# Attention units two at a time in every second group of the expert stream, with two buffers for their magnitudes

## The reference, cut to what matters

```
# stick-breaking attention, block i of 128 queries, keys 0 .. kv_len
z = einsum('bhqd,bhkd->bhqk', q_i, k_i) * scale
log_fail = where(mask, -softplus(z), 0.0)
later_fail = cumsum(log_fail, axis=3, reverse=True) - log_fail
w = where(mask, exp(log_sigmoid(z) + later_fail), 0.0)
outs.append(einsum('bhqk,bhkd->bhqd', w, v_i))
...
# experts, one block of 128 tokens; idx holds 128 experts for each token
u = expert_u[idx]
act = gelu(einsum('thkd,td->thk', u, tb))
return einsum('thk,thkd->td', g * act, expert_v[idx])
```

## Time and profile before

| what | value |
|---|---|
| median of the runs | 3309.58 us |
| the profiled execution: its own time | 3309.43 us |
| its span, first to last instruction | 3307.6 us |
| granted TensorE clock, mean | 0.959 |
| PE busy, share of the span | 2857.1 us, 86% |
| DVE, ACT, POOL busy | 2026.9, 1498.7, 1310.7 us |
| HBM traffic over the span | 345 GB/s |

### The profile page before, as it was taken

How to read it: one execution, slowest core, us unless ns; L and a number is a source line. 1 busy time by engine, 2 the same in 40 slices (tenths; PEclk the granted TensorE clock), 3 DMA queues, 4 the chain that set the end, 5 groups by cost and what they waited for, 6 DMA issues and landing times.

```text
span 3307.6 us, 33642 instructions
## 1 busy us (share of the span) xinstructions
PE 2857.1 (86%) x8606; PEld 1370.9 (41%) x8606; DVE 2026.9 (61%) x4767; ACT 1498.7 (45%) x3712; POOL 1310.7 (40%) x1134
## 2 busy tenths in 40 slices
PE   8899779997999879997999879998997689777776
PEld 5668634433453334433453334433452235322222
DVE  2111684895559655785559655795559655975444
ACT  3151153784446633674448733685332333232222
POOL 1000134544444434443444534444343444345553
PEclk9999889998999999998999989999998899999999
DMA  3541499999999999989998999989999899999998
GB/s 111 174 126 56 153 356 392 387 333 368 381 420 341 342 375 399 389 322 383 386 419 331 334 364 386 397 322 357 381 422 383 366 407 400 400 403 387 421 421 335
DMA packets 200267, 1143.70 MB, mean 346 GB/s; under 512 B 23585, under 2 KB 59761, under 8 KB 68737
## 3 DMA queue, kind: packets, MB, share of 16 engines
q0 software_dynamic: 147456, 1073.81, 81.7%
q1 hardware_dynamic: 52608, 67.67, 6.2%
HBM read 1126.31 MB, written 15.07 MB: 345 GB/s over the span
## 4 chain that ended last, share of the span: by engine, by line
PE 40%; DVE 23%; DMA 18%; issue 8%; ACT 6%; POOL 3%; POOLq 0%; DVEq 0%; SPq 0%; ACTq 0%
PE ps L1482 20%; DMA r_uv<-in_experts,r_wk 17%; DVE r_uv L1156 9%; PE ps L1260 5%; PE ps L1436 3%; PE ps L1419 3%; POOL r_uv L609 3%; PE ps L1221 2%; DVE r_wk L1094 2%; DVE r_wk L1092 1%; DVE r_wk L1095 1%; DVE r_wk L1000 1%; DVE r_wk L1003 1%; DVE r_wk L1009 1%; PE ps L1290 1%
## 5 line engine op out<-in xcount | busy, mean ns | idle before, releaser
L1482 PE MATMUL ps<-r_uv,r_wk 128*128 128x512 f32 x4096 | 1956.2, 622 | 376.2 <-ACT r_wk L838 371.4
L609 POOL DMA_INDIRECT r_uv<-in_experts,r_wk x1024 | 1199.2, 1171 | 1716.3 <-PE ps L1482 1385.5
L1156 DVE CUSTOM_DVE_ANT_0 r_uv<-r_uv,hncur 128x1024 f32<-128x1024 f32 x1024 | 1251.0, 1242 | 736.4 <-DMA r_uv<-in_experts,r_wk 726.0
L1482 PEld LDWEIGHTS ps<-r_uv,r_wk 128*128 128x128 f32 x4096 | 767.0, 196 | 1390.5 <-issue 877.8
L828 ACT ACTIVATE r_wk<-r_wk 128x2 f32<-128x2 f32 x512 | 104.4, 204 | 1294.3 <-DVE r_wk L1156 1292.6
L838 ACT ACTIVATE r_wk<-cst,r_wk 128x128 f32<-128x128 f32 x1024 | 356.0, 395 | 100.4 <-PE ps L1482 56.3
L834 ACT ACTIVATE r_wk<-r_wk 128x1 f32<-128x1 f32 x1024 | 246.2, 288 | 17.2
L828 ACT ACT_TABLE_LOAD x151 | 193.7, 1283 | 19.0 <-issue 16.4
L637 ACT ACT_TABLE_LOAD x147 | 188.6, 1283 | 6.6 <-PE ps L1412 1.9
L1436 PEld LDWEIGHTS ps<-r_wk,r_wq 128*128 128x128 f32 x1024 | 123.8, 192 | 27.0 <-issue 26.8
L1436 PE MATMUL ps<-r_wk,r_wq 128*128 128x128 f32 x1024 | 124.0, 275 | 0.0
(11 more groups left out here) (155 smaller groups left out, 2035.8 us busy)
## 6 DMA issues: line engine op xcount, KB each, us to landing
r_uv<-in_experts,r_wk POOLq DMA_INDIRECT x1024
r_wk<-lkv_dram SPq DMA_DIRECT2D x72, 128.0 KB
r_uv<-in_x SPq DMA_DIRECT2D x8, 512.0 KB, 3.6
hncur<-in_w_chunks SPq DMA_DIRECT2D x8, 512.0 KB, 3.9
h2cur<-in_w_chunks SPq DMA_DIRECT2D x8, 512.0 KB, 3.8
fnb<-in_w_chunks SPq DMA_DIRECT2D x8, 512.0 KB, 4.4
r_wo<-in_w_out SPq DMA_DIRECT2D x8, 512.0 KB, 5.1
r_wk<-in_x SPq DMA_DIRECT2D x8, 512.0 KB
```

What stands on the lines that cost most here:

```text
L609: g.indirect_dma_start(uv[:, k % NB, :], None, experts, bass.IndirectOffsetOnAxis(idxcur_u[:, k:k + 1], 0)).then_inc(rows_in[k % NB], 16)
L1156: v.tensor_tensor_reduce(uv[:, k % NB, 0:D], uv[:, k % NB, 0:D], hncur[:, :], 1.0, 0.0, ALU.mult, ALU.add, actv[:, k:k + 1]).then_inc(dott ...
L1482: last = t_.matmul(ps[:, i, :], diag[:, k % 4, :], uv[:, k % NB, D + 512 * i:D + 512 * i + 512], start=k == 0, stop=k == K - 1)
```

## The change

`LATE_AT` now starts two units in the same group, and the next two two groups later. In numbers: units 0 to 19 of block 0 started in groups 34, 35, 36, 37, 38, 40, ... 56 and start in 34, 34, 36, 36, ... 52, 52; in blocks 1 and 2 the 14 units end in group 46 in place of 56, in blocks 3 and 4 the 18 units end in group 50 in place of 56. `laz` becomes two buffers, chosen by u % 2, so ACT may write the logs of a unit while DVE has not yet read those of the one before. The room for it comes from a new buffer of 512 words and from letting `pos` and `posf` share theirs (the conversion is done in place).

```
-LATE_AT = {f: [34 + 24 * u // len(units) for u in range(len(units))] for f, (g, units) in LATE.items()}
+LATE_AT = {f: [34 + 2 * (u // 2) for u in range(len(units))] for f, (g, units) in LATE.items()}
...
-        pos = grid(pos_v.bitcast(U32), PH)
+        pos = grid(posf_v.bitcast(U32), PH)
...
+        laz1_v = sb("laz1", 512)
         laz_v, lw0_v = parts(qT_v, [512, 512])
-        laz = grid(laz_v, 2)
+        laz = (grid(laz_v, 2), grid(laz1_v[:, :], 2))
...
             def late_logs(b, first, u):
-                if u >= 1:
-                    gate(act, "act", lsp_ready, ub + u)
+                if u >= 2:
+                    gate(act, "act", lsp_ready, ub + u - 1)
                 act.wait_ge(lz_ready, ub + u + 1)
-                unit_logs(u, laz[0:r, :, c0:GW], bank(u, r, c0))
+                unit_logs(u, laz[u % 2][0:r, :, c0:GW], bank(u, r, c0))
...
             def late_softplus(b, first, u):
-                softplus(u, lsp[0:r, u % 2, :, :], laz[0:r, :, c0:GW], bank(u, r, c0), c0, own_)
+                softplus(u, lsp[0:r, u % 2, :, :], laz[u % 2][0:r, :, c0:GW], bank(u, r, c0), c0, own_)
```

More of the change, by code:

```diff
@@ L241, in block_program @@
         small = sb("small", 64)
-        r_wk = sb("r_wk", 13216)
+        r_wk = sb("r_wk", 13088)
         (pT_v, ssb_v, sq_v, qT_v, hs, hnn, in_v, topv_v, topi_v, topf_v, cs_v, ci_v,
-         lw1_v, tops_v, pos_v, posf_v, idxf, idxn, gn, actv, gel, idxcur, gcur, diag_v) = parts(r_wk, [
+         lw1_v, tops_v, posf_v, idxf, idxn, gn, actv, gel, idxcur, gcur, diag_v) = parts(r_wk, [
              2048, 2048, D, D, D, D, 512 + P + 512, 256, 256, 256, PH * NC, PH * NC,
-             512, K, K, K, K, K, K, K, K, K, K, 4 * P])
+             512, K, K, K, K, K, K, K, K, K, 4 * P])
         TOP_AT = 2 * 2048 + 4 * D + 512 + P + 512
```

## The result

The changed kernel takes 3379.6 us (median of 4 runs, 3376.1 to 3382.9) against 3311.6 us for the kernel before on the same chip: a ratio of 1.0205, 95% interval 1.0187 to 1.0223. The forecast was 3343.5 us, its own range 3318 to 3370, and the wide range up to rival C 3304 to 3383. The direction was right; 34.1 us more were forecast and 68.0 came, so the forecast was half of it and the measured time lies above its own range. The profiled execution took 3382.93 us, 73.5 us more than that of before. All lines after the change have moved down by one (L1290 is L1291).

What follows compares the result with a forecast made beforehand. PE was taken as the bound, shared with DVE in blocks 1 and 2. Blocks 0 to 4 changed by +13.3, -1.3, +1.6, +10.2 and +10.3, together 34.1 us on 3309.4: 3343.5 us, range 3318 to 3370, wide 3304 to 3383.

Steps and rivals of the forecast that it cites:

- rival C: Groups 41 to 49: DVE waits for ACT's second logs, 40 us more, 3383 us; chance 0.10.
- the loads: ACT's table loads: 127 of 298 go, 163 us of ACT's time, not counted as gains by themselves.
- the trip: Between two neighbouring PE sums, PE waits for POOL's addition: 36 times, 1.05 to 1.92 us each, together 62.9 us.
- may find POOL still issuing a gather: Upper bound on one PE wait for POOL's addition, which may stand behind a gather's issue: some 2.5 us.
- from PE's busy time: Blocks 1 to 4: sums start from PE's busy time, 154.9, 155.9, 168.3 and 168.6 us, leaving out its idle time.
- the tails: Groups after the last unit, partly at the gathers' pace: 3.9 us lost in blocks 1 and 2, 1.5 in 3 and 4.
- my upper bound: Most that groups after the last unit could lose: 11.7 us in blocks 1 and 2, 5.6 in 3 and 4.
- The eight buffers are full when PE comes out of its full stretch: After the last unit, saved-up gathers let part of the groups run at PE's 3.54 us instead of 4.46 to 4.71.
- A: Table switches counted and PE's waits for POOL are short: idle time in blocks 1 to 4 goes, 3296 us; chance 0.11.
- B: Gains and waits cancel, PE's waits for POOL falling into time given to DVE: 3303 to 3316 us; chance 0.11.

Runs made afterwards that it cites:

- e5: The changed kernel with a pair of table switches put back into the groups between; 3368.2 us, ratio 1.0176.
- e15: The changed kernel with the first unit's later sum on PE moved in front of the group's second k; 3497.6 us, ratio 1.0559.
- e16: e15 with POOL's additions also moved in front of the gather behind that k; 3342.1 us, ratio 1.0101.
- e4: The changed kernel with one unit in every group from 34 on instead of two in every second; 3300.5 us, ratio 0.9969.
- e11: e4 with the last six units of blocks 1 and 2 in every second group; 3306.1 us, ratio 0.9992.
- e14: The kernel before, one laz buffer, with a unit in every group from 34 on as its one edit; 3300.9 us, ratio 0.9959.
- e7: The kernel before with only the second laz buffer and the shared pos, units in their old places; 3311.0 us, ratio 1.0003.
- e1: The changed kernel with PE's second sum of a couple moved behind the weighs and second-head scores; 3357.6 us, ratio 1.0147.
- e18: e1 with SP's store of a pair's output two units later; 3349.6 us, ratio 1.0114.
- e12: The changed kernel with POOL's additions cut into pieces of 32 columns; 3542.3 us, ratio 1.0683.

## Why the prediction was right in direction and half in size

**Right: the loads.** 81 and 90, ACT 163 us less by them, worth nothing: forecast and measured. e5 is the test.

**Right: the trip, its number and place.** 36 waits, 69.9 us for 62.9. The sizes differ within: a copy 1.18 or 1.44 us (forecast 1.05), an undisturbed full addition 1.59 (1.92), and eleven of the 36 between 2.2 and 3.9. Timeline of block 3 of the kernel after, first PE, then POOL, the same place in the units' work as the earlier trace rows:

```profile
1779.68 1.02 PE L1297 MATMUL ps<-r_wk,cst 128*128 128x512 f32 x2
1782.30 1.10 PE L1291 MATMUL ps<-r_wk,cst 128*128 128x512 f32 x2 [1.59 <-POOL r_wk L575]
```

```profile
1779.80 0.94 POOL L610 DMA_INDIRECT r_uv<-in_experts,r_wk  x1 [2.03 <-PE ps L1483]
1780.89 1.26 POOL L575 TENSOR_TENSOR r_wk<-r_wk 128x512 f32<-128x512 f32 x1 [0.15 <-PE ps L1297]
```

In all 36 trips of that execution a gather's issue stands right in front of the addition and ends at most 0.15 us before it. Where it takes 0.94 us it is just over when PE's sum ends; where it is late or takes longer, PE waits for it too. The prediction had named that case ("may find POOL still issuing a gather") as a bound; e15 and e16 show that it is part of the trip.

**Wrong: what was set against the trips.** The sum was started "from PE's busy time", so the 39.6 us of idle time in blocks 1 to 4 was booked as gone, and in its stead stood the tails at 3.9 + 3.9 + 1.5 + 1.5 = 10.8 us. The units' part came out well in sum: 691.5 us of PE's work (818.9 less 36 tail groups at 3.54) and 62.9 of trips make 754.4, measured 758.6. By block some of that is luck: block 0 was 9.5 us over, with PE's busy time up by 8 us at a clock of 0.92, and blocks 1 and 2 together 9.3 under. The tails were to take 127.4 + 10.8 = 138.2 us and took 174.0: 19.2, 48.8, 48.5, 28.6 and 28.9. These 36 us more are nearly all of the 39 that the forecast lacked; PE is idle for 38.6 us in the tails, where 10.8 were booked. Even my upper bound, 34.6 us over PE's pace, was too low by 12. "The eight buffers are full when PE comes out of its full stretch, so part of the tail runs at PE's pace" was the sentence that failed: the tail groups ran at 4.8 to 4.9 us each with DMA at 1.01. The trace shows why. PE and then POOL of the kernel after, block 1, and a window between:

```profile
1109.02 7.77 PE L1483 MATMUL ps<-r_uv,r_wk 128*128 128x512 f32 x16
1116.72 1.23 PE L1304 MATMUL ps<-r_wk 128*64 128x256 f32 x8
1117.88 7.13 PE L1483 MATMUL ps<-r_uv,r_wk 128*128 128x512 f32 x16
1126.75 5.42 PE L1483 MATMUL ps<-r_uv,r_wk 128*128 128x512 f32 x12 [1.73 <-ACT r_wk L839]
```

```profile
1100.59 0.94 POOL L610 DMA_INDIRECT r_uv<-in_experts,r_wk  x1 [0.79 <-PE ps L1483]
...
1112.46 0.98 POOL L610 DMA_INDIRECT r_uv<-in_experts,r_wk  x1 [9.09 <-PE ps L1483]
```

```profile
1108.00:1111.00 3.00, 3.00 (x9) 1.27 (x6) 2.93 (x5) 2.05 (x3) 0.00 (x0) 0.61 0.24 98
```

The eight buffers are indeed full, but earlier: at about 1110 us, behind the units' work of group 48, when POOL stands 9.09 us for a free buffer and the DMA engines fall to 0.24. From 1109.02 PE takes exactly eight k without a wait and then waits. Six of the eight stand in groups 49 to 51, inside the units' part, whose groups had been booked at PE's pace anyway; two are left for the tail that starts at group 52 (1121.42). When that group starts, DVE has done the dots of these two k and of none behind them. Blocks 2, 3 and 4 show the same eight k and a first wait of 1.73 us. e4 shows nearly the same tails (165.1 us) without a single couple, and e4, e11, e14 and e7 all keep PE's idle time at 38 to 44 us, wherever they put the units. I can show that it is kept in these placings; that it must be is not shown.

**Smaller terms.** Against e4, which has the same density, the change costs 81 us in the stretches: 69.9 of trips, 9.6 of busy time at a lower clock (0.92 to 0.97 by stretch against 0.99 to 1.00), 1.5 for keys. The closeness alone, for which the tails stood in the sum, is worth 8 us to the good.

**The rivals.** A (3296 us) and B (3303 to 3316) are out. C's time, 3383 us, is the one measured, but not by its mechanism: after the change PE doesn't wait for DVE at all in the stretches. Yet its chain exists. With the trips gone PE waits 29.1 us for DVE in e16, and e1, e16 and e18, all nearly without trips, lie at 3342 to 3358 us, 42 to 57 above e4. So taking the trips away gives only 22 to 38 of their 70 us, and in the accounts 18 to 24 us of that is busy time at a higher clock. That the trips hid the chain is how I read it; what the couples cost beyond the trips I have by difference, and which of DVE, ACT's diagonals and keys sets it first isn't told apart.

## What to carry to other kernels

When an engine is full in one part of a loop and paced by transfers in another, do not subtract an added wait from its idle time: first find out in which part that idle time lies, since waiting added to the full part is paid on top. Two steps of a chain through another engine cost nothing while enough other work stands between them, and a full round trip once they are neighbours, and the round trip includes whatever stands in front of the answer in the other engine's order. Here the version to keep is one unit a group with one buffer (ratio 0.9959), an edit of one line that couples no units at all.

## What the runs showed of the hardware

**POOL stands still beside DVE's two-operand work.** POOL and DVE of the kernel after, block 1:

```profile
1040.65 2.08 POOL L575 TENSOR_TENSOR r_wk<-r_wk 128x512 f32<-128x512 f32 x1 [0.15 <-PE ps L1297]
```

```profile
1040.62 0.99 DVE L1095 TENSOR_TENSOR r_wk<-r_wk 128x800 f32<-128x800 f32 x1
```

The addition takes 2.08 us instead of 1.27 when it begins beside DVE's. Of the 32-column pieces of e12, 490 that began beside no DVE instruction took 0.25 us (0.28 at most), 63 that began beside the stream's dot (L1158, two operands) had a median of 1.23 us, the length of a dot. The Trainium skill (SBUF — State Buffer, "Who interferes with whom") has this rule: a VectorE instruction with two inputs in SBUF contends with a GpSimd instruction that reads SBUF. The trace agrees: the pieces beside the dot took 1.23 us, the dot itself 1.22. What I had not expected is that the issue of a gather is held too: in the kernel after, 393 issues beside no DVE instruction took 0.94 us (1.12 at most), 392 beside a dot had a median of 1.55 and 2.60 at most. In eight of the eleven trips of 2.2 us or more, the gather's issue (1.68 to 1.82 us) or POOL's addition was lengthened so.

**Longer waits came with a lower granted clock.** After a wait of 1.59 us the sum ran in 1.10 us (the rows at 1782.30 above), at the full level of 2.4 GHz. After one of 3.86 us in block 0 everything ran at half of that, 1.2 GHz, for the rest of the group. PE of the kernel after:

```profile
733.56 1.02 PE L1291 MATMUL ps<-r_wk,cst 128*128 128x512 f32 x2
...
739.30 2.05 PE L1291 MATMUL ps<-r_wk,cst 128*128 128x512 f32 x2 [3.86 <-POOL r_wk L575]
741.14 1.91 PE L1297 MATMUL ps<-r_wk,cst 128*128 128x512 f32 x2
```

Over that group (728.77 to 746.80 us) the granted clock was 0.76. The length of one wait does not decide it: after 2.42 us at 1042.88 the sum ran in 1.10 us, after 2.40 at 1451.73 in 2.05. In the five stretches 109.6 us more waiting in e12 came with 51.8 us more busy time, while the 69.9 us of the change itself, in shorter waits, came with 9.6 us more than in e4. That the waits are the cause is argued from this, not shown apart.
